# Three products of half-length chunk sets in place of one product of all chunks, and page loads moved from POOL to SP

## The chip, the cores and the metric

The kernel runs on one core of a Trainium2 chip. The metric is the device time of one execution in microseconds (us), as the median of three runs. TensorE is PE, VectorE DVE, ScalarE ACT, GpSimd POOL and SyncE SP in what follows. All arithmetic is in float32; PE takes a float32 product in two passes, and the profile lists each pass as one MATMUL with its LDWEIGHTS.

## The reference, cut to what matters

One step of a hybrid decoder layer: projection, retention, sparse attention for a prompt of 1024 tokens and for 8 sampled tokens (each with 2048 past tokens in 16 pages of a cache), output projection, feed-forward. What the change touches is the compression of the cached rows: blocks of 32 tokens that start every 16 tokens go through a small network, for keys (k) and values (v).

```python
def compress(rows, pos_emb, w1, w2):
    L = rows.shape[0]
    nb = (L - CMP_BLK) // CMP_STRIDE + 1
    idx = np.arange(nb)[:, None] * CMP_STRIDE + np.arange(CMP_BLK)[None, :]
    blk = rows[idx] + pos_emb[None, :, None, :]
    blk = blk.transpose(0, 2, 1, 3).reshape(nb, KV_GROUPS, CMP_BLK * HEAD_DIM)
    return jax.nn.gelu(blk @ w1) @ w2
```

The compressed keys give scores, from whose softmax the best blocks of each sequence are chosen; the selected rows (`selk`, `selv`), the window rows and the compressed rows are then attended to.

## The kernel before, in words

The program has six stages, one after the other. Only `stage_sequences` is changed; it is followed by `stage_attention` (the prompt's attention), the output projection and the feed-forward stage.

`stage_sequences` works on nine sequences q: q = 0 is the prompt (64 chunks of 16 tokens, 63 blocks), q = 1 to 8 the samples (128 chunks, 127 blocks). It is written out by hand as a software pipeline of eleven steps, 0 to 10 (`STEPS_B`), in which each engine has its own fixed list of instructions, tied by semaphores. In step s PE does, in this order:

- `compress(s, 0)`: the keys' compression of sequence s. Sixteen transposes (`turn_rows`, L1066) bring the chunks' rows into PSUM in four parts i, ACT copies each part into `XT` (`keep_turned`, L1219), and PE multiplies it with the weights `w1` (L1085): 32 products of 254 columns, 64 passes, for q = 0 of 126 columns. Block n is chunk n times the lower half of `w1` plus chunk n+1 times the upper half. ACT then makes the gelu (L1228), and PE the second layer (`compressed`, L1106 and L1111), which comes early in the next sequence's `compress`.
- `values(s-2)`: transposes of the weights of the softmax (L1120), `first_keys` (L1142), and 21 products with the selected and window values (L1129); it signals `pv_done`.
- `scores(s-1)`: transposes of the selected keys (L1142) and the scores (L1165).
- `compress(s, 1)`, the same for values, with `importance(s-1)` (L1171) in its middle.

After `importance`, DVE ranks the blocks (L1417 to L1433) and takes a maximum (L1437); then ACT takes two exponentials (L1240, L1250), DVE scales (L1381, L1384, signal `b_scaled`), and `values` of the next step may start.

The pages come by DMA. In step s SP waits for `pv_done` of sequence s-2 and loads the window values (L951, L953), waits for the last key transpose and loads 16 pages of `selk` (L916, 64 KB each), then the window keys (L959), then reads the 16 page numbers of sequence s+2 into registers (L936), waits until POOL has regrouped the blocks before, and loads that sequence's 16 pages of 128 KB into `cmpb` (L916). POOL loads the 16 pages of `selv` (L983, `load_values`) and regroups `cmpb` into `cmpg` (L1003). In step 0 SP also loads the retention state of the samples and a table of constants. After the last step SP loads `kstage` (L966) and the queries (L846) for the next stage.

At the start DVE also normalizes the prompt's retention output (L1316 to L1325), and, once the state and the constants are there, computes the samples' retention (L1330 to L1347), which needs a square root by ACT (L1282) in its middle.

## Time and profile before

| what | value |
|---|---|
| median of 3 runs | 2133.79 us (2131.57 to 2135.72) |
| the profiled execution | 2134.98 us, its span 2133.3 us |
| PE busy over the span | 94% |
| DVE, ACT, POOL busy | 38%, 30%, 28% |
| `stage_sequences` | from 461.6 to 942.4 us of the span |

A row of the trace gives start, duration, engine, line, operation, what it writes and reads, and how many instructions were merged; in brackets the idle time of the engine before it and what ended it. The trace's granted clock of PE is 1.00 at its upper level, 2.4 GHz, and 0.50 at its lower, 1.2 GHz.

### The profile page before, as it was taken

To read this page: it belongs to the slowest core of one execution; us is meant where nothing else is said; L and a number is where in the kernel's file an instruction comes from. 1 tells how busy PE (TensorE), PEld (TensorE's weight loads), DVE (VectorE), ACT (ScalarE), POOL (GpSimd) and SP (SyncE) were. 2 spreads that over 40 slices of the span, in tenths; PEclk is the share of its full clock that TensorE was granted. 3 is DMA by queue.
4 is the path that set the end of the run, shared out by engine and by line. 5 is a ranking of instruction groups with operands and counts; after the bars stand their busy time and mean duration, and the time that the engine had idled before them with its cause. 6 is when DMAs were issued, how large, how long until landed. Compare 5 with 4: busy or idle time off the path is not lost. (4 is left out here: it accounts for less than half of the span.)

```text
span 2133.3 us, 32535 instructions
## 1 busy us (share of the span) xinstructions
PE 1997.9 (94%) x11749; PEld 1729.3 (81%) x11749; DVE 817.4 (38%) x1590; ACT 637.6 (30%) x1290; POOL 600.0 (28%) x628
## 2 busy tenths in 40 slices
PE   6999989977999999869999989899999999999997
PEld 4777767855777777647778868699999999999987
DVE  5634443454354344467777843101111101110115
ACT  4301111212233334356777843222101111111112
POOL 0111111211232222154545731133322323223330
PEclk9999989988999999979999989999999999999999
DMA  6121101247786784470000032211111111111113
GB/s 182 42 89 40 40 12 61 81 133 117 109 110 97 102 100 66 57 154 13 11 11 21 2 99 90 70 49 44 45 49 49 39 49 43 45 49 49 45 64 120
DMA packets 173848, 141.33 MB, mean 66 GB/s; under 512 B 16601, under 2 KB 160682, under 8 KB 173410
## 3 DMA queue, kind: packets, MB, share of 16 engines
q1 hardware_dynamic: 169634, 131.43, 26.9%
q0 software_dynamic: 4096, 8.40, 2.6%
q8 instruction: 66, 1.08, 0.2%
q14 instruction: 52, 0.43, 0.1%
HBM read 124.27 MB, written 19.69 MB: 67 GB/s over the span
## 5 line engine op out<-in xcount | busy, mean ns | idle before, releaser
L392 PE MATMUL banks<-halves 128*128 128x344 f32 (+4 forms) x5184 | 855.1, 327 | 14.4 <-POOL halves L401 14.4
L392 PEld LDWEIGHTS banks<-halves 128*128 128x128 f32 (+1 forms) x5184 | 820.6, 188 | 44.8 <-POOL halves L401 7.7
L401 POOL TENSOR_TENSOR halves<-core,halves 128x1024 fp32r<-128x1024 f32 (+1 forms) x143 | 243.9, 1713 | 574.9 <-ACT halves L397 425.0
L392 PE MATMUL banks<-hidden 128*128 128x512 f32 (+3 forms) x1512 | 349.4, 387 | 9.0 <-DVE hidden L401 9.0
L392 PEld LDWEIGHTS banks<-hidden 128*128 128x128 f32 (+1 forms) x1512 | 254.5, 179 | 77.5 <-issue 9.7
L1085 PE MATMUL banks<-arena,blocks 128*128 128x254 f32 (+1 forms) x1152 | 248.2, 372 | 9.1 <-ACT arena L1219 5.1
L1085 PEld LDWEIGHTS banks<-arena,blocks 128*128 128x128 f32 x1152 | 209.4, 194 | 34.4 <-issue 6.1
L397 ACT ACTIVATE halves<-core 128x1024 fp32r<-128x1024 f32 (+1 forms) x85 | 88.1, 1047 | 390.3 <-PE banks L392 369.6
L2063 DVE TENSOR_TENSOR core<-banks,core 128x344 f32<-128x344 f32 x66 | 34.1, 517 | 440.4 <-PE banks L392 440.4
L1653 POOL TENSOR_SCALAR arena<-arena,kept 128x64 f32<-128x64 f32 (+8 forms) x192 | 123.3, 654 | 129.3 <-DVE arena L1705 127.2
L983 POOL DMA_DIRECT2D arena<-in_cache_kv x128 | 67.9, 530 | 232.6 <-PE banks L1129 206.0
L1694 DVE TENSOR_REDUCE arena<-banks 128x1 f32<-128x64 f32 (+8 forms) x184 | 101.6, 557 | 61.7 <-PE banks L1577 58.1
L1619 ACT ACTIVATE arena<-banks,arena 128x64 f32<-128x64 f32 (+8 forms) x192 | 109.3, 570 | 47.9 <-DVE arena L1694 46.4
L1573 PEld LDWEIGHTS banks<-pairs 128*128 128x128 f32 x592 | 98.9, 197 | 25.0 <-ACT arena L1619 16.2
L1573 PE MATMUL banks<-pairs 128*128 128x128 f32 (+3 forms) x592 | 105.4, 310 | 9.8 <-ACT arena L1619 9.1
L1601 PE MATMUL banks<-pairs 128*128 128x512 f32 (+1 forms) x296 | 106.2, 440 | 3.4 <-ACT arena L1640 3.4
L1586 PE MATMUL banks<-core,arena 128*128 128x128 f32 (+1 forms) x592 | 94.0, 282 | 11.1 <-DVE pairs L401 10.1
L596 POOL TENSOR_TENSOR retention<-core,retention 128x256 f32<-128x256 f32 (+1 forms) x36 | 30.3, 842 | 261.6 <-ACT core L579 261.6
L401 DVE TENSOR_TENSOR pairs<-banks,pairs 128x512 fp32r<-128x512 f32 (+1 forms) x148 | 99.2, 678 | 10.4 <-ACT pairs L397 10.3
L397 ACT ACTIVATE pairs<-banks 128x512 fp32r<-128x512 f32 (+1 forms) x148 | 88.0, 594 | 41.4 <-PE banks L1586 40.6
L1219 ACT ACTIVATE arena<-banks 128x512 f32<-128x512 f32 (+1 forms) x72 | 39.5, 574 | 151.7 <-PE banks L1066 151.2
L664 DVE TENSOR_TENSOR retention<-core,retention 128x128 f32<-128x128 f32 (+1 forms) x72 | 37.6, 564 | 119.9 <-ACT core L579 119.9
(209 smaller groups left out, 1884.6 us busy)
## 6 DMA issues: line engine op xcount, KB each, us to landing
core<-in_cache_kv SPq DMA_DIRECT2D x128, 128.0 KB, 5.3
core<-in_w_gate SPq DMA_DIRECT2D x22, 512.0 KB, 3.7
core<-in_w_up SPq DMA_DIRECT2D x22, 512.0 KB, 3.8
core<-in_x_prompt SPq DMA_DIRECT2D x16, 512.0 KB, 3.4
arena<-in_cache_kv SPq DMA_DIRECT2D x128, 64.0 KB, 6.0
arena<-in_cache_kv POOLq DMA_DIRECT2D x128, 64.0 KB, 5.1
retention<-in_w_in SPq DMA_DIRECT2D x16, 448.0 KB, 6.3
core<-in_w_down SPq DMA_DIRECT2D x16, 448.0 KB, 3.7
```

The lines of the kernel that those rows point to most:

```text
L392: done = pe.matmul(out, left[a], right[b], start=(first and i == 0), stop=(last and i == 2))
L397: return act.activation(hi, x, ACT.Copy)
L401: return engine.tensor_tensor(lo, x, hi.bitcast(F32), ALU.subtract)
L983: pool.dma_start(m.selv[16 * at:16 * at + 16, half, :, :], io.pool[bass.ds(page[pg], 1), :, :, 384:512].rearrange("a c t n -> (a c) t n")) ...
L1085: last = pe.matmul(m.banks[:, 2 + mt, 0:2 * nb], m.w1[kv][:, k, P * mt:P * mt + P], m.XT[:, k % 8, :, k // 8:k // 8 + nb], start=(k == 0), ...
L1219: act.activation(m.XT.rearrange("p (h j) g c -> p j h g c", h=2)[:, i, :, :, 0:nch], m.banks[:, u % 2, :].rearrange("p (g c h) -> p h g c" ...
L1573: last = pe.matmul(out[:, lo:hi], m.qs[t % 2][:, g, hh, :], pair[v][:, first + lo:first + hi], start=(v == 0), stop=(v == 1 and not mask))
L1586: last = pe.transpose(m.banks[0:w, 4 + i % 3, P * hh:P * hh + P], m.prob[(4 * k + hh) % 12][:, P * x:P * x + w], m.ident)
L1601: last = pe.matmul(m.banks[:, 7, :], v.rearrange("p v d -> p (v d)"), m.pts[i % 3][half][0:w, :], start=(br == 0 and half == 0), stop=(br ...
L1619: act.activation(m.prob[u % 12][:, 0:n], scores_of(u), ACT.Exp, bias=m.nmax[:, u % 8:u % 8 + 1], accum_out=m.sums[t % 2][:, u % PER_TILE:u ...
L1653: pool.tensor_scalar(p, p, m.share[t % 2][:, u % PER_TILE:u % PER_TILE + 1], m.gates[:, tile_at(t), gate:gate + 1], ALU.mult, ALU.mult).th ...
L1694: dve.tensor_reduce(peak, scores_of(u), AX.X, ALU.max, negate=True).then_inc(s["c_max"], 1)
```

## The change

It computes the first layer with three products of half as many columns. The chunks are split into even and odd ones. With L and U the lower and upper half of the weights, p1 = odd x L and p0 = even x U, and both = (even + odd) x (L + U). Even blocks are both - p1 - p0, odd blocks p1 plus p0 shifted by one chunk. POOL makes L + U once per kind (`weight_sum`) and even + odd in four parts per sequence and kind (`chunk_sums`), PE makes 48 products of 128 columns (of 64 for q = 0), ACT copies the three results from PSUM to SBUF (`keep_apart`), DVE combines them (`summed`), and ACT makes the gelu from SBUF. Compressed blocks are stored with even ones first, and the mask and the importance sums follow that order. The 16 loads of `selv` go from POOL to SP, behind the window values and ahead of `selk`. On DVE the normalization's second half (`norm_gate`) goes behind the samples' retention; on ACT the square root goes ahead of the copies of `compress(0, 1)`; on PE `compressed` and `importance` go further back in `compress`.

```diff
@@ -94,7 +94,7 @@
-    n = np.arange(64)
+    n = 2 * (np.arange(64) % 32) + np.arange(64) // 32
...
@@ -256,13 +256,16 @@
-    m.XT = b(2048).rearrange("p (j g c) -> p j g c", j=8, g=2)
+    m.XT = b(2048)
+    m.both = b(1024).rearrange("p (j g c) -> p j g c", j=8, g=2)
+    m.w1sum = [e(2048).rearrange("p (k n) -> p k n", k=8) for _ in range(2)]
+    m.apart, m.hidden = e(768), e(512).rearrange("p (e n) -> p e n", e=2)
...
@@ -882,6 +885,12 @@
+    even, odd = (m.XT[:, 1024 * e:1024 * e + 1024].rearrange("p (j g c) -> p j g c", j=8, g=2) for e in range(2))
+
+    def products(ap, q):
+
+        return ap.rearrange("p (a c) -> p a c", c=64)[:, :, 0:chunks_of(q) // 2]
...
@@ -951,6 +960,7 @@
                     sp.dma_start(m.winv, io.wins[q - 1, :, :].rearrange("(p t) n -> p t n", t=4)[:, :, 128:256]
                                  ).then_inc(s["last_values_in"], 16)
                     sp.dma_start(m.vcb[q % 2][127:128, :], io.kvs[q - 1:q, 384:512]).then_inc(s["last_values_in"], 16)
+                    pages(q, m.selv, 384, 128, "values_in")
...
@@ -971,38 +981,45 @@
-            def load_values(q):
-                for pg in range(NPG):
-                    half, at = divmod(pg, NPG // 2)
-                    pool.dma_start(m.selv[16 * at:16 * at + 16, half, :, :],
-                                   io.pool[bass.ds(page[pg], 1), :, :, 384:512].rearrange("a c t n -> (a c) t n")
-                                   ).then_inc(s["values_in"], 16)
...
+            def regroup(q, kv):
+                n = CH if q else HCH
+                if q:
+                    pool.wait_ge(s["cmp_in"], 16 * NPG * q)
+                    pool.wait_ge(s["b_turned"], TURN_AT["kv"[kv], q - 1, 3] + 1)
+                pool.tensor_copy(m.cmpg[:, kv, :, 0:n, :],
+                                 m.cmpb.rearrange("p h t n -> p (h t) n")[:, 0:n, P * kv:P * kv + P]
+                                 .rearrange("p t (g d) -> p g t d", g=2)).then_inc(s["b_grouped"], 1)
+
+            def weight_sum(kv):
+                pool.wait_ge(s[f"b_w_in{kv}"], 48 if kv else 128)
+                pool.tensor_tensor(m.w1sum[kv], m.w1[kv][:, 0:8, :], m.w1[kv][:, 8:16, :], ALU.add).then_inc(s["b_w_sum"], 1)
+
+            def chunk_sums(q, kv):
+                mc = chunks_of(q) // 2
+                for i in range(4):
+                    pool.wait_ge(s["b_kept_act"], kept_by(TURN_AT["kv"[kv], q, i] + 1, False))
+                    out, x0, x1 = (x.rearrange("p (h j) g c -> p j h g c", h=2)[:, i, :, :, 0:mc] for x in (m.both, even, odd))
+                    pool.tensor_tensor(out, x0, x1, ALU.add).then_inc(s["b_both"], 1)
 
             pool.wait_ge(s["cmp_early"], 16)
...
-                if q >= 3:
-                    load_values(q - 2)
...
+            regroup(0, 0)
+            regroup(0, 1)
+            pool.wait_ge(s["b_w_first"], 64)
+            weight_sum(0)
+            for step in STEPS_B:
+                for kv in range(2):
+                    if step in SEQS_B and (step or kv == 0):
+                        chunk_sums(step, kv)
+                    if step == 0 and kv == 0:
+                        weight_sum(1)
+                        chunk_sums(0, 1)
+                    if step == 2 and kv == 0:
+                        pool.wait_ge(s["b_kc_kept"], 1)
+                        nb = chunks_of(0) - 1
+                        rest_to_lo(pool, m.kcbP[:, :, 1, 0:nb], m.kcb[0].rearrange("p (g n) -> p g n", g=2)[:, :, 0:nb],
+                                   m.kcbP[:, :, 0, 0:nb]).then_inc(s["b_kcp_lo"], 1)
+                    if step + 1 in SEQS_B:
+                        regroup(step + 1, kv)
...
@@ -1066,29 +1083,47 @@
+                def product(bank, at, w, x, j, mt, first):
+                    out = m.banks[:, bank, at:at + P].rearrange("p (g c) -> p g c", g=2)[:, :, 0:mc]
+                    return pe.matmul(out, w[:, P * mt:P * mt + P], x[:, j, :, 0:mc], start=first, stop=(j == 7),
+                                     skip_group_check=True)
+
+                def shared(i):
+                    if q == 0 and i == 0:
+                        pe.wait_ge(s["b_w_sum"], kv + 1)
+                    pe.wait_ge(s["b_both"], 8 * q + 4 * kv + i + 1)
+                    for j in (i, 4 + i):
+                        for mt in range(2):
+                            last = product(3, P * mt, m.w1sum[kv][:, j, :], m.both, j, mt, j == mt == 0)
+                    return last
+
+                mc = nch // 2
                 turn_rows(0)
                 turn_rows(1)
-                if kv == 0 and q:
-                    compressed(q - 1)
-                done = 2 * q + kv
-                if q == 0 and kv:
-                    pe.wait_ge(s["b_w_in1"], 48)
-                wait(pe, "b_gelu", 2 * done)
+                wait(pe, "b_apart", 2 * (2 * q + kv))
                 for i in range(4):
                     if i in (1, 2):
                         turn_rows(i + 1)
-                    if done == 0 and i % 2 == 0:
+                    if q == 0 and i == 0 and kv:
+                        pe.wait_ge(s["b_w_in1"], 48)
+                    if q == 0 and i % 2 == 0 and kv == 0:
                         pe.wait_ge(s["b_w_in0" if i else "b_w_first"], 128 if i else 64)
                     pe.wait_ge(s["b_kept_act"], kept_by(TURN_AT["kv"[kv], q, i] + 1, False))
-                    for k in (i, 4 + i, 8 + i, 12 + i):
+                    for j in (i, 4 + i):
                         for mt in range(2):
-                            last = pe.matmul(m.banks[:, 2 + mt, 0:2 * nb], m.w1[kv][:, k, P * mt:P * mt + P],
-                                             m.XT[:, k % 8, :, k // 8:k // 8 + nb], start=(k == 0), stop=(k == 15))
-                    if i == 0 and kv == 1 and 1 <= q - 1:
+                            product(2, P * mt, m.w1[kv][:, j, :], odd, j, mt, j == mt == 0)
+                            last = product(2, 256 + P * mt, m.w1[kv][:, 8 + j, :], even, j, mt, False)
+                    if i == 3:
+                        last.then_inc(s["b_apart_done"], 1)
+                    if i:
+                        shared(i - 1)
+                    if i == 1 and kv == 0 and q:
+                        compressed(q - 1)
+                    if i == 1 and kv == 1 and 1 <= q - 1:
                         if 1 <= q - 2:
                             turn_output(q - 2)
                         importance(q - 1)
-                last.then_inc(s["b_hidden"], 1)
+                shared(3).then_inc(s["b_hidden"], 1)
                 if q == 0:
                     position_bias(kv)
...
@@ -1210,23 +1245,34 @@
-                nch = chunks_of(q)
+                mc = chunks_of(q) // 2
-                    act.activation(m.XT.rearrange("p (h j) g c -> p j h g c", h=2)[:, i, :, :, 0:nch],
-                                   m.banks[:, u % 2, :].rearrange("p (g c h) -> p h g c", g=2, h=2)[:, :, :, 0:nch],
+                    act.activation(m.XT.rearrange("p (x j g c) -> p j x g c", x=4, j=4, g=2)[:, i, :, :, 0:mc],
+                                   m.banks[:, u % 2, :].rearrange("p (g c x) -> p x g c", g=2, x=4)[:, :, :, 0:mc],
                                    ACT.Copy).then_inc(s["b_kept_act"], 1)
 
+            def keep_apart(q, kv):
+                n = 2 * q + kv
+                act.wait_ge(s["b_apart_done"], n + 1)
+                wait(act, "b_summed", n)
+                act.activation(products(m.apart[:, 0:512], q), products(m.banks[:, 2, :], q), ACT.Copy).then_inc(s["b_apart"], 1)
+                act.wait_ge(s["b_hidden"], n + 1)
+                act.activation(products(m.apart[:, 512:768], q), products(m.banks[:, 3, 0:256], q), ACT.Copy
+                               ).then_inc(s["b_apart"], 1)
-                act.wait_ge(s["b_hidden"], 2 * q + kv + 1)
+                mc = chunks_of(q) // 2
+                act.wait_ge(s["b_summed"], 2 * q + kv + 1)
-                    act.activation(m.G[kv][:, mt, 0:2 * nb], m.banks[:, 2 + mt, 0:2 * nb], ACT.Gelu_apprx_tanh,
-                                   bias=m.cbias[:, 2 * mt + kv:2 * mt + kv + 1]).then_inc(s["b_gelu"], 1)
+                    act.activation(m.G[kv][:, mt, 0:4 * mc].rearrange("p (g e c) -> p g e c", g=2, e=2),
+                                   m.hidden[:, :, P * mt:P * mt + P].rearrange("p e (g c) -> p g e c", g=2)[:, :, :, 0:mc],
+                                   ACT.Gelu_apprx_tanh, bias=m.cbias[:, 2 * mt + kv:2 * mt + kv + 1]
+                                   ).then_inc(s["b_gelu"], 1)
...
@@ -1252,7 +1298,12 @@
                 if step == 0:
                     keep_bias(0)
                 if step in SEQS_B:
+                    keep_apart(step, 0)
                     gelu(step, 0)
+                if step == 0:
+                    act.wait_ge(s["r_ssum"], 1)
+                    act.activation(rms, ss, ACT.Sqrt, bias=m.small[0:NR, 64:65], scale=1.0 / HD
+                                   ).then_inc(s["r_srms"], 1)
...
@@ -1274,13 +1325,12 @@
                     keep_turned(q, 1, range(2 if 1 <= q - 1 <= NB_SEQ else 0, 4))
                     if q == 0:
                         keep_bias(1)
+                    keep_apart(q, 1)
+                    if q + 1 in SEQS_B:
+                        keep_turned(q + 1, 0, range(2))
                     gelu(q, 1)
                     if q + 1 in SEQS_B:
-                        keep_turned(q + 1, 0)
-                    if q == 0:
-                        act.wait_ge(s["r_ssum"], 1)
-                        act.activation(rms, ss, ACT.Sqrt, bias=m.small[0:NR, 64:65], scale=1.0 / HD
-                                       ).then_inc(s["r_srms"], 1)
+                        keep_turned(q + 1, 0, range(2, 4))
...
@@ -1311,41 +1361,71 @@
-            for hp in range(4):
+            dve.memset(m.hidden, 0.0).then_inc(s["b_cleared"], 1)
+            dve.wait_ge(s["b_cleared"], 3)
+
+            def summed(q, kv):
+
+                n, last = 2 * q + kv, chunks_of(q) // 2 - 1
+                dve.wait_ge(s["b_apart"], 2 * n + 2)
+                wait(dve, "b_gelu", 2 * n)
+                p1, p0, both = (products(m.apart[:, 256 * x:256 * x + 256], q) for x in range(3))
+                first, second = (products(m.hidden[:, e, :], q) for e in range(2))
+                dve.tensor_tensor(second[:, :, 0:last], p1[:, :, 0:last], p0[:, :, 1:last + 1], ALU.add)
+                own.after(dve.tensor_tensor(first, both, p1, ALU.subtract))
+                dve.tensor_tensor(first, first, p0, ALU.subtract).then_inc(s["b_summed"], 1)
+
+            def norm_sums(hp):
...
-            for hp in range(4):
+
+            def norm_gate(hp):
...
+
+            def sample_out():
+                dve.wait_ge(s["const_in"], 48)
+                dve.wait_ge(s["r_rows_in"], 32)
...
+                dve.tensor_reduce(ss, prod, AX.X, ALU.add).then_inc(s["r_ssum"], 1)
+
+            def sample_state():
...
+                dve.wait_ge(s["r_srms"], 1)
+                own.after(dve.reciprocal(rstd, rms))
+                dve.scalar_tensor_tensor(out=ro, in0=ro, scalar=rstd, in1=rg, op0=ALU.mult, op1=ALU.mult
+                                         ).then_inc(s["r_o"], 1)
+                dve.scalar_tensor_tensor(out=S0, in0=S0, scalar=m.gone[0:NR, :], in1=S2, op0=ALU.mult,
+                                         op1=ALU.add).then_inc(s["r_new_state"], 1)
...
+            for hp in range(4):
+                norm_sums(hp)
+            sample_out()
+            summed(0, 0)
+            sample_state()
+            summed(0, 1)
+            for hp in range(4):
+                norm_gate(hp)
             dve.wait_ge(s["r_gated"], 4)
-
...
+            summed(1, 0)
+            summed(1, 1)
...
@@ -1382,6 +1462,8 @@
                     dve.tensor_scalar(SR[:, SEL], SR[:, SEL], bst[:, 8:9], None, ALU.mult).then_inc(s["b_scaled"], 1)
+                    if step in SEQS_B:
+                        summed(step, 0)
                     dve.wait_ge(s["pt_done"], q)
...
@@ -1397,6 +1479,8 @@
                         keep_output(q)
+                if step == 2:
+                    summed(2, 0)
                 q = step - 1
...
@@ -1434,6 +1518,8 @@
                     own.after(added)
+                    if step in SEQS_B:
+                        summed(step, 1)
                     dve.tensor_reduce(bst[:, 5:6], SR[:, SEL], AX.X, ALU.max, negate=True).then_inc(s["b_sel_max"], 1)
 
 

```

In the listings of order below the line numbers are those of each kernel. First ACT, at the start of `stage_sequences`, from the bias of the keys on. Before (L1196 and L1198 the bias, L1228 gelu, L1219 `keep_turned`, L1282 the square root):

```order
L1196 ACTIVATE arena<-banks 1x256
L1198 ACTIVATE arena<-banks 128x2
L1228 ACT_TABLE_LOAD
L1228 ACTIVATE arena<-banks,arena 128x126 x2
L1219 ACTIVATE arena<-banks 128x2x2x64 x4
L1196 ACTIVATE arena<-banks 1x256
L1198 ACTIVATE arena<-banks 128x2
L1228 ACTIVATE arena<-banks,arena 128x126 x2
L1219 ACTIVATE arena<-banks 128x2x256 x4
L1282 ACT_TABLE_LOAD
L1282 ACTIVATE core<-core 64x1
```

Now ACT at the same place (L1262 and L1264 `keep_apart`, L1272 gelu, L1305 the square root, L1254 `keep_turned`):

```order
L1231 ACTIVATE arena<-banks 1x256
L1233 ACTIVATE arena<-banks 128x2
L1262 ACTIVATE blocks<-banks 128x8x32
L1264 ACTIVATE blocks<-banks 128x4x32
L1272 ACT_TABLE_LOAD
L1272 ACTIVATE arena<-blocks,arena 128x128 x2
L1305 ACT_TABLE_LOAD
L1305 ACTIVATE core<-core 64x1
L1254 ACTIVATE arena<-banks 128x4x2x32 x4
```

The gelu of `compress(0, 0)` now waits for DVE's `summed(0, 0)`, and it and the square root stand ahead of the four copies that `compress(0, 1)` multiplies.

Now DVE at the same place, behind the four pairs of `norm_sums` (L1395 to L1406 `sample_out`, L1374 to L1376 `summed(0, 0)`, L1409 the start of `sample_state`):

```order
L1395 TENSOR_SCALAR core<-core 64x64
L1396 TENSOR_TENSOR core<-core 64x64
L1397 TENSOR_REDUCE core<-core 64x1
L1398 TENSOR_SCALAR core<-core 64x64
L1400 TENSOR_TENSOR arena<-arena,core 64x4096
L1402 TENSOR_REDUCE core<-arena 64x64
L1403 SCALAR_TENSOR_TENSOR core<-core,arena 64x64
L1405 TENSOR_TENSOR core<-core 64x64
L1406 TENSOR_REDUCE core<-core 64x1
L1374 TENSOR_TENSOR blocks<-blocks 128x4x31
L1375 TENSOR_TENSOR blocks<-blocks 128x4x32
L1376 TENSOR_TENSOR blocks<-blocks 128x4x32
```

The whole of `sample_out` stands ahead of `summed(0, 0)`; before, nothing that the compression waits for stood on DVE.

## Rows read from the trace of the kernel before

**Rows 1.** Groups by line and shape; 40 us of steady steps: busy PE, PEld, DVE, ACT, POOL, clock.

```profile
L1085 PE MATMUL banks<-arena,blocks 128*128 128x254 f32 x1024 | 230.4, 381 | 3.4 <-ACT arena L1219 3.4
...
L1219 ACT ACTIVATE arena<-banks 128x512 f32<-128x512 f32 x64 | 36.6, 598 | 128.7 <-PE banks L1066 128.3
...
700.00:740.00 40.00, 38.66 (x227) 28.89 (x226) 21.28 (x34) 17.28 (x30) 12.65 (x18) 1.00 0.78 94
```

**Rows 2.** PE in order of time: passes of 254 and 126 columns, transposes and their weight loads.

```profile
731.30 7.02 PE L1085 MATMUL banks<-arena,blocks 128*128 128x254 f32 x32
...
474.40 3.73 PE L1085 MATMUL banks<-arena,blocks 128*128 128x126 f32 x32
...
720.67 0.86 PEld L1066 LDWEIGHTS banks<-core,blocks 128*128 128x128 f32 x8 [0.86 <-issue]
```

**Rows 3.** The start of the stage, in order of time: DVE, ACT, PE.

```profile
487.40 0.62 ACT L1228 ACTIVATE arena<-banks,arena 128x126 f32<-128x126 f32 x2
496.19 7.07 PE L1025 MATMUL banks<-blocks,arena 128*1 128x256 f32 x32
512.05 1.94 PE L1066 MATMUL banks<-core,blocks 128*128 128x128 f32 x8 [8.06 <-issue]
517.42 0.19 DVE L1330 TENSOR_SCALAR core<-core 64x64 f32<-64x64 f32 x1 [29.89 <-DMA arena<-in_const]
518.42 7.30 DVE L1335 TENSOR_TENSOR arena<-arena,core 64x4096 f32<-64x4096 f32 x1
530.76 0.21 DVE L1341 TENSOR_REDUCE core<-core 64x1 f32<-64x64 f32 x1
```

**Rows 4.** Stretch by stretch: the granted clock (0.51) after PE has stood for 8 us.

```profile
512.00:521.00 9.00, 8.95 (x35) 7.94 (x36) 3.44 (x5) 1.20 (x2) 1.79 (x1) 0.51 0.73 180
```

**Rows 5.** SP's DMA issues over one step.

```profile
714.13 0.60 SPq L951 DMA_DIRECT2D core<-out  x1
718.17 11.76 SPq L916 DMA_DIRECT2D arena<-in_cache_kv  x16
729.97 0.60 SPq L959 DMA_DIRECT2D core<-out  x1
740.34 11.86 SPq L916 DMA_DIRECT2D core<-in_cache_kv  x16
763.03 0.60 SPq L951 DMA_DIRECT2D core<-out  x1
```

**Rows 6.** POOL's issues and regrouping in that step, DVE beside it, a POOL addition by group.

```profile
714.79 9.80 POOL L983 DMA_DIRECT2D arena<-in_cache_kv  x16 [29.80 <-PE banks L1129]
724.59 1.90 POOL L1003 COPY blocks<-core 128x2048 f32<-128x2048 f32 x1
...
724.71 1.87 DVE L1409 TENSOR_SCALAR core<-arena,core 8x127 f32<-8x127 f32 x1
...
L596 POOL TENSOR_TENSOR retention<-core,retention 128x256 f32<-128x256 f32 x32 | 26.7, 833 | 234.3 <-ACT core L579 234.3
```

**Rows 7.** Time to landing of the pages that SP loads, from the DMA part of the page.

```profile
core<-in_cache_kv SPq DMA_DIRECT2D x128, 128.0 KB, 5.3
```

**Rows 8.** The last sequence: from the products' end to `pv_done`.

```profile
616.14 0.38 PE L1165 MATMUL banks<-core,kept 128*8 128x128 f32 x2
...
861.46 0.58 SPq L951 DMA_DIRECT2D core<-out  x1
...
893.87 2.40 PE L1120 MATMUL banks<-core,arena 8*128 8x8 f32 x21 [6.34 <-DVE arena L1384]
...
903.68 0.59 SPq L951 DMA_DIRECT2D core<-out  x1
```

**Rows 9.** The end of the stage.

```profile
904.83 4.97 SPq L966 DMA_DIRECT2D core<-turned_keys  x8
...
920.36 3.89 ACT L397 ACTIVATE pairs<-core 128x1024 fp32r<-128x1024 f32 x4
924.15 1.99 ACT L1250 ACTIVATE arena<-arena,core 8x2049 f32<-8x2049 f32 x1
```

More of the change, by code:

```diff
@@ L280, in place_mixer @@
     m.rrow = x(512)
-    m.G = [b(508).rearrange("p (m n) -> p m n", m=2) for i in range(2)]
+    m.G = [b(512).rearrange("p (m n) -> p m n", m=2) for i in range(2)]
     m.brow = b(256)
@@ L973, in _ @@
         def _(pool):
-            def load_values(q):
-                page = [pool.value_load(m.pages[0:1, x:x + 1], min_val=0, max_val=NPOOL - 1)
-                        for x in range(NPG * (q - 1), NPG * q)]
-                if q == 1:
-                    pool.wait_ge(s["r_new_state"], 1)
-                wait(pool, "pv_done", q - 1)
-                for pg in range(NPG):
-                    half, at = divmod(pg, NPG // 2)
-                    pool.dma_start(m.selv[16 * at:16 * at + 16, half, :, :],
-                                   io.pool[bass.ds(page[pg], 1), :, :, 384:512].rearrange("a c t n -> (a c) t n")
-                                   ).then_inc(s["values_in"], 16)
@@ L1334, in _ @@
-            dve.wait_ge(s["r_state_in"], 16)
-            own.after(dve.tensor_tensor(S2v, S0v.rearrange("p d e -> p e d"), rq.unsqueeze(1).broadcast_to(S2v.shape),
-                                        ALU.mult))
-            own.after(dve.tensor_reduce(qs, S2v, AX.X, ALU.add))
-            own.after(dve.scalar_tensor_tensor(out=ro, in0=qs, scalar=m.gone[0:NR, :], in1=ro, op0=ALU.mult,
-                                               op1=ALU.add))
-            own.after(dve.tensor_tensor(prod, ro, ro, ALU.mult))
@@ new lines, in sample_state @@
+            def sample_state():
+                own.after(dve.tensor_tensor(S2v, rk8.unsqueeze(2).broadcast_to(S2v.shape),
+                                            rv.unsqueeze(1).broadcast_to(S2v.shape), ALU.mult))
+                dve.wait_ge(s["r_srms"], 1)
[4 more added lines that the diff above has]
+                                         op1=ALU.add).then_inc(s["r_new_state"], 1)
```

52 lines of the change are left out of this document (16 added, 36 removed).

## The prediction, made blind

> **What bounds the kernel now.** I read the groups by line first, to find which engine `stage_sequences` waits for. In 40 us of steady steps PE is busy for 38.66 us at the full clock, DVE for 21.28, ACT for 17.28, POOL for 12.65 [rows 1]. So PE sets the pace of these steps, and the passes of the first layer (1024 of them) are the largest piece of its work. PE in order of time gives their real spacing, which the mean of 381 ns in the group does not, since passes overlap: 32 passes of 254 columns take 7.02 us, so one takes 0.2145 us once the last one's tail is taken off [rows 2]. Then SP in order of time: one step lasts from 714.13 to 763.03, 48.9 us, and SP's first issue in it comes as soon as `pv_done` is there [rows 5]. The start and the end of the stage are different: there PE stands, for the first sample's blocks [rows 3] and for DVE and ACT at the last sequence [rows 8]. They have to be followed one by one.
>
> **The passes.** A `compress` of a sample had 64 passes of 254 columns, 13.7 us. It now has 96 of 128. The nearest row is 32 passes of 126 columns in 3.73 us, 0.111 us each [rows 2]; with two more columns 0.112, so 96 take 10.7 us. The gain is 3.0 us each, 48 us over sixteen. From below the stream of 128 columns can't be under half of 0.2145, which would give 10.3 us; from above I allow 0.125, 12 us. For q = 0 it is the other way: 64 passes of 126 columns took 7.1 us, 96 of 64 columns each still load 128 columns of weights, and a load takes 0.106 us (eight in 0.86 us) [rows 2], so I take 0.11, 10.6 us: 3.5 us more each, where PE is waited for at all.
>
> The rows of 126 columns show the load running beside the stream: 0.111 us holds a load of 0.106 and a stream of 0.105. The Trainium skill, page "TensorE: Matmul & The Clock Gate", section "The mechanism", says that a weight load overlaps running products only where the row groups differ. By that rule the new passes would cost the sum, about 0.21 us, and sixteen `compress` would lose 6.7 us each instead of gaining 3.0. The row is against it.
>
> **The start.** This is where I expect the largest single loss. DVE could begin the samples' retention only at 517.42, when the constants had landed, and came to the end of what is now `sample_out` at 530.76 + 0.21 = 530.97 [rows 3]. Nothing in the change brings that data earlier: SP issues it behind the first sample's pages, as before. Now `summed(0, 0)` stands behind `sample_out` on DVE, the gelu of `compress(0, 0)` waits for it, and on ACT the gelu and the square root stand ahead of the copies for `compress(0, 1)`. ACT issues in order, so PE gets no part of `compress(0, 1)` until then. Step by step: three small DVE operations to 531.9 (0.3 each); gelu 0.6 (before, 0.62 [rows 3]); a table load of 1.28 and the root 0.3; the first copy 0.4: 534.4. Before, that gelu ran at 487.40. Then `compress(0, 1)`: PE has stood for 40 us. After the 8.06 us of standing before 512.05, the clock stood at 0.51 for the next 9 us [rows 3, 4]; so 9 us of the passes go at half speed (41 passes), the other 55 take 6.1 us, transposes 0.4: 550. The bias takes 7.07 [rows 3] and 0.9 for its copies: `compress(1, 0)` begins at 558.0 instead of 512.05, **46 us later**. The wait for the first pages (8.06) and POOL's weight sums are hidden in this.
>
> **From there to the first `pv_done`.** It stood at 616.3 [rows 8]. Five `compress` lie between, 15.0 us less. The slow 9 us after 512.05 cost 4.3 and are not paid again. New waits: `compress(1, 1)` follows at once, and its first copy stands behind PSUM copies (0.5), `summed` (1.2) and gelu (0.8) on ACT, 2.5 us; `scores(1)` waits 1.0 for `summed(2, 0)`; 0.4 at each start of a `compress(s, 0)` for `keep_apart`: 4.7 together. So `pv_done` of sequence 1 comes at 616.3 + 46 - 15.0 - 4.3 + 4.7 = 647.7.
>
> **A steady step by PE alone** would be 48.9 - 2 x 3.0 + 0.2 = 43.1 us. The copies (0.60 for 512 columns [rows 1]) and POOL's additions (0.83 for 256 columns [rows 6], four per `compress`) fit beside 1.8 us of passes per part.
>
> **SP's step.** From the first load of `selk` at 718.17 to the end of the `cmpb` issues at 752.20 SP has no wait on PE: 34.0 us, of which 9.8 are the reading of page numbers between 730.57 and 740.34 [rows 5]. The window values add 1.2. The change adds 16 issues of the kind that took 11.76 us. That is 34.0 + 1.2 + 11.8 = **47.0 us in a step**, more than PE's 43.1: SP becomes the pace-setter as long as it still has `cmpb` to load, in steps 3 to 6. It starts level (its step 2 ends at about 645), so `cmpb` of sequence 8 is issued by 647.7 + 4 x 47.0 = 835.7. The last page lands 5.3 us after its issue [rows 7], 4.6 after that; regrouping takes 1.90, the first addition 0.83 [rows 6]: 843.0. The wait is felt at the first shared product of `compress(7, 1)`, because on POOL the regrouping of sequence 8 stands ahead of the additions for it; that product lies 12.4 us behind `pv_done` of sequence 5, which is thus at 830.6 in effect, and `pv_done` of sequence 6 at 830.6 + 43.1 = 873.7. Before, it was at 861.4 [rows 8].
>
> What POOL is relieved of, 9.80 us of issues [rows 6], was waited for by nobody: `selv` is used 30 us later. The Trainium skill, page "SBUF — State Buffer", section "SBUF: two separate sides", warns that DVE copies stop DMAs issued from POOL and advises issuing them elsewhere. By that rule the move is a gain; the sum would be the same by it, less at most a few us at the last sequence, where nothing waits for these loads either.
>
> **The last sequence.** From `pv_done` 6 to `pv_done` 7 took 903.68 - 861.46 = 42.2 us [rows 8], with PE waiting 6.34 us for DVE at the end. The saved passes don't help: the ranking starts 1.1 us later (`importance` stands further back), `summed(8, 1)` adds 1.2 to it, and the gelu comes just behind. I get the same 42.2: 915.9, 12.2 us later than before.
>
> **The end.** SP issued `kstage` right behind the window values, at 904.83 for 4.97 us; ACT rounded it at 920.36 for 3.89 us and made the last exponential at 924.15 [rows 9]. Now 11.8 us of `selv` issues stand ahead: issued up to 18.0 us after `pv_done`, landed at 23.5, rounded by 27.4, exponential from there, against 20.5 before. **6.8 us** that nothing covers; the values that DVE and POOL prepare for the next stage hang on it.
>
> **Sum:** 12.2 + 6.8 = 19.0 us on the profiled execution's 2134.98, 2154.0. The profiled one is 1.2 above the median, so I forecast a median of **2153 us**. The later stages have the same work.
>
> **The rivals.**
> - SP does not set the pace: an issue of `selv` is cheaper than one of `selk`, or the page numbers are read faster. Then the five steps take 43.1: 647.7 + 5 x 43.1 + 42.2 = 905.4, 1.7 later than before, and with the end 2143.5. Against it: the 16 issues took the same 0.74 us each for 64 and 128 KB [rows 5]. 14%.
> - The start is covered, the other sign: `compress(0, 1)` does not wait for `sample_out`. It decides at 487.4, when PE would take the first copy. Then `pv_done` 1 is at about 604. With SP's pace SP is then at 628 after step 2 and `cmpb` 8 at 816, and the end comes out at -7 + 7: 2135. With PE's pace it is 604 + 215.5 + 42.2 = 861.7, 42 earlier, 2100. For it only that the data might land sooner; the order rows speak against it. 5% and 4%.
> - It is worse by contention: an operation of 0.27 us on DVE took 1.87 beside POOL's copy [rows 6], and POOL now works beside DVE's ranking and `summed`. With 2 us more in each of seven steps the sum is 2168. 15%.
> - Loads don't hide behind passes of 128 columns. Sixteen times 6.7 instead of -3.0 puts it at 2134 + 46 + 107, less what the start saved, about 2280. 1%, since the row of 126 columns is so near.
>
> **How the numbers follow.** The forecast has the other 61%, with a range of its own of 2146 to 2162 from 0.107 to 0.125 a pass (half of it hidden behind SP) and 46 to 48.5 for SP's step. The range of 8 in 10 reaches to the second and the fourth case: 2138 to 2169. About 4 us, 0.2%, is what a measurement can tell: faster 5%, the same 8%, slower 87%.
>
> **What the changed profile would show.** PE idle from about 492 to 534, ending at an ACT copy; 96 passes per `compress` at 0.112 us; SP issuing without a gap between 648 and 836, and `pv_done` every 47 us; PE waits of some 4 us at `compress(s, 1)` for POOL's additions; ACT waiting for `kstage` at the end. I am wrong if PE doesn't stand at 490, or if SP waits for `pv_done` in steps 4 to 6.

## The result and the profile after

| what | value |
|---|---|
| the changed kernel | 2184.99 us, median of 4 runs (2184.33 to 2187.1) |
| the kernel before, on the same chip | 2134.76 us (2131.57 to 2137.15) |
| ratio | 1.0238, 95% interval 1.022 to 1.0256 |
| span of the profiled execution | 2185.3 us (before 2133.3) |

The change makes the kernel 50 us slower. I had forecast slower, but by 19 us (2153, range 2138 to 2169): the direction is right and the size is not.

In the rows of the changed kernel L1083 are the transposes of `turn_rows`, L1088 the passes of the first layer, L1042 the bias, L1254 the copies of `keep_turned`, L1002 POOL's additions (`chunk_sums`), L989 its regrouping and L925 the page loads.

The groups by line and shape from 560 to 700 us of the changed kernel:

```profile
L1088 PE MATMUL banks<-arena,blocks 128*128 128x128 f32 x672 | 79.0, 276 | 4.8 <-ACT arena L1254 4.8
L1254 ACT ACTIVATE arena<-banks 128x512 f32<-128x512 f32 x28 | 15.9, 593 | 24.6 <-PE banks L1083 24.2
```

The windows (busy PE, PEld, DVE, ACT, POOL, then the granted clock, the DMA share and GB/s):

```profile
482.00:494.00 12.00, 12.00 (x59) 12.00 (x57) 0.00 (x0) 2.57 (x6) 4.91 (x2) 0.50 0.07 17
544.00:556.00 12.00, 12.00 (x58) 11.90 (x56) 0.00 (x0) 0.39 (x1) 4.12 (x3) 0.50 0.45 65
574.40:580.00 5.60, 5.60 (x52) 5.60 (x51) 5.50 (x5) 1.67 (x5) 4.56 (x2) 1.00 0.29 86
760.00:800.00 40.00, 33.69 (x276) 31.45 (x275) 21.12 (x34) 14.45 (x26) 11.40 (x10) 0.87 0.60 92
```

Beside [rows 1] the last window is the one to look at: there PE is no longer busy throughout, and its clock is 0.87 instead of 1.00. It is the worst of the steady steps; from 700 to 760 and from 800 to 855 us the clock is 0.97.

The waits of PE over this stage, as in the list of waits (us in total, times, longest):

```profile
PE banks L1088 <- ACT arena L1254: 38.2, 17, 29.7
PE banks L1155 <- issue: 17.1, 1, 17.1
PE banks L1088 <- POOL arena L1002: 14.2, 5, 5.1
PE banks L1141 <- ACT arena L1272: 7.6, 5, 4.9
```

The start in order of time on PE; it answers to [rows 2, 3]:

```profile
504.33 0.66 PE L1083 MATMUL banks<-core,blocks 128*128 128x128 f32 x4 [0.26 <-ACT arena L1233]
534.73 3.65 PE L1088 MATMUL banks<-arena,blocks 128*128 128x64 f32 x16 [29.75 <-ACT arena L1254]
...
544.04 12.05 PE L1088 MATMUL banks<-arena,blocks 128*128 128x64 f32 x56
556.01 8.90 PE L1042 MATMUL banks<-blocks,arena 128*1 128x256 f32 x32
...
565.92 1.09 PE L1083 MATMUL banks<-core,blocks 128*128 128x128 f32 x8 [0.26 <-ACT arena L1233]
```

And on DVE and ACT:

```profile
474.06 1.22 DVE L1381 TENSOR_REDUCE core<-arena 128x16 f32<-128x1024 f32 x1
517.89 0.19 DVE L1395 TENSOR_SCALAR core<-core 64x64 f32<-64x64 f32 x1 [42.62 <-DMA arena<-in_const]
...
531.19 0.27 DVE L1374 TENSOR_TENSOR blocks<-blocks 128x124 f32<-128x124 f32 x1
...
532.02 0.69 ACT L1272 ACTIVATE arena<-blocks,arena 128x128 f32<-128x128 f32 x2 [25.86 <-DVE blocks L1376]
```

DVE stood for 42.62 us for the constants, with the first `summed` (L1374) queued behind them in program order; ACT stood for that sum, and PE for ACT. PE took up work at 534.73.

SP over one step, which answers to [rows 5]:

```profile
806.12 1.06 SPq L960 DMA_DIRECT2D core<-out  x1
807.23 0.51 SPq L962 DMA_DIRECT2D core<-out  x1
807.92 25.06 SPq L925 DMA_DIRECT2D arena<-in_cache_kv  x32
833.03 0.60 SPq L969 DMA_DIRECT2D core<-out  x1
843.41 11.85 SPq L925 DMA_DIRECT2D core<-in_cache_kv  x16
855.30 0.60 SPq L960 DMA_DIRECT2D core<-out  x1
```

There is no gap but the reading of page numbers (833.63 to 843.41), so SP does not wait for `pv_done` in this step. L960 comes at 658.66, 708.68, 757.04, 806.12 and 855.30, 49.2 us a step. Behind SP's last `cmpb` issue come POOL and PE:

```profile
862.75 1.89 POOL L989 COPY blocks<-core 128x2048 f32<-128x2048 f32 x1 [27.99 <-DMA core<-in_cache_kv]
864.60 2.08 POOL L1002 TENSOR_TENSOR arena<-arena 128x256 f32<-128x256 f32 x3
```

```profile
865.37 2.07 PE L1088 MATMUL banks<-arena,blocks 128*128 128x128 f32 x8 [3.81 <-POOL arena L1002]
869.00 8.70 PE L1088 MATMUL banks<-arena,blocks 128*128 128x128 f32 x56
```

The data is there at 862.75; PE then stands 3.81 us for an addition of the present sample, queued behind the regrouping of the next, and its 56 passes take 8.70 us instead of 6.42 after that stop. The end:

```profile
900.49 0.58 SPq L960 DMA_DIRECT2D core<-out  x1
945.52 0.58 SPq L960 DMA_DIRECT2D core<-out  x1
959.72 5.07 SPq L976 DMA_DIRECT2D core<-turned_keys  x8
...
971.15 3.89 ACT L400 ACTIVATE pairs<-core 128x1024 fp32r<-128x1024 f32 x4 [9.05 <-DMA core<-turned_keys]
```

ACT waits 9.05 us for `kstage`.

### The profile page after: what moved, and what is told of

Read it like the earlier page. It is cut to its first block and busy times, and to the rows that moved or that the text cites. A ratio compares the mean times of both kernels' runs of the same rounds, so it can differ in the third digit from the quotient of the medians.

```text
span 2185.3 us, 33508 instructions
## 1 busy us (share of the span) xinstructions
PE 1994.9 (91%) x12325; PEld 1746.4 (80%) x12325; DVE 846.3 (39%) x1645; ACT 654.5 (30%) x1326; POOL 599.6 (27%) x574
## 5 line engine op out<-in xcount | busy, mean ns | idle before, releaser
L1088 PE MATMUL banks<-arena,blocks 128*128 128x128 f32 (+1 forms) x1728 | 229.5, 297 | 57.1 <-ACT arena L1254 38.2
L1088 PEld LDWEIGHTS banks<-arena,blocks 128*128 128x128 f32 x1728 | 223.1, 212 | 61.9 <-issue 41.7
L1659 PEld LDWEIGHTS banks<-pairs 128*128 128x128 f32 x592 | 100.1, 200 | 24.4 <-ACT arena L1705 15.6
L1002 POOL TENSOR_TENSOR arena<-arena 128x256 f32<-128x256 f32 (+1 forms) x72 | 58.7, 829 | 208.0 <-ACT arena L1254 208.0
L2100 ACT ACTIVATE core<-banks 128x344 f32<-128x344 f32 x66 | 30.3, 460 | 175.0 <-PE banks L395 174.9
```

What stands on the lines that cost most here:

```text
L1002: pool.tensor_tensor(out, x0, x1, ALU.add).then_inc(s["b_both"], 1)
L1088: return pe.matmul(out, w[:, P * mt:P * mt + P], x[:, j, :, 0:mc], start=first, stop=(j == 7), skip_group_check=True)
L1659: last = pe.matmul(out[:, lo:hi], m.qs[t % 2][:, g, hh, :], pair[v][:, first + lo:first + hi], start=(v == 0), stop=(v == 1 and not mask))
```

## The experiments

Theory: the loss is made by queues, not by products. DVE's at the start, SP's in the middle and at the end, and POOL's where additions stand behind a regrouping. Rival: the three-product form costs it by itself (clock, contention, copies, sums). Twelve kernels separate them. Ratios are to the kernel before, measured on the same chip as each; its medians there lay between 2135.1 and 2137.0. Line numbers shift by some between kernels.

| run | median us | ratio (interval) |
|---|---|---|
| e1_start | 2188.09 | 1.0249 (1.0219 to 1.0279) |
| e2_pool_values | 2191.79 | 1.0256 (1.0223 to 1.029) |
| e3_both | 2199.61 | 1.0295 (1.0264 to 1.0325) |
| e4_sp_only | 2143.56 | 1.0036 (1.0021 to 1.005) |
| e5_wide | 2176.91 | 1.0197 (1.0171 to 1.0223) |
| e6_regroup_late | 2177.45 | 1.0207 (1.0181 to 1.0234) |
| e8_start3 | 2153.65 | 1.0089 (1.0063 to 1.0115) |
| e10_start3_late | 2148.95 | 1.0062 (1.0041 to 1.0083) |
| e9_start3_pool_late | 2132.81 | 0.9986 (0.9973 to 0.9999) |
| e12_start3_pool | 2163.65 | 1.0137 (1.0116 to 1.0159) |
| e11_all_wide | 2136.08 | 1.0003 (0.999 to 1.0017) |
| e13_all_wide2 | 2127.28 | 0.9958 (0.9941 to 0.9975) |

### e1: another order at the start

```diff
-            sample_out()
             summed(0, 0)
-            sample_state()
             summed(0, 1)
             for hp in range(4):
                 norm_gate(hp)
+            sample_out()
+            sample_state()
             summed(1, 0)
```

The square root on ACT goes back behind the copies of `compress(1, 0)`.

> The changed kernel with the start in another order: on DVE summed(0, 0), summed(0, 1) and the four norm_gate stand ahead of sample_out, and ACT's square root goes back behind the copies of compress(1, 0). If ACT's wait for sample_out holds PE at the start, the wait of 29.75 us before the first passes of compress(0, 1) is gone and compress(1, 0) begins about 33 us earlier (near 533 instead of 565.9). If SP sets the pace behind that, not all of it comes out at the end: SP's chain of loads can only start some 20 to 24 us earlier, so the median falls from 2185 to about 2162. If SP does not set the pace, all 33 come out: 2152. If PE stands at the start for another reason, nothing changes: 2185.

2188.09: a miss. PE in order of time:

```profile
504.28 2.61 PE L1088 MATMUL banks<-arena,blocks 128*128 128x64 f32 x16 [2.29 <-ACT arena L1254]
...
534.95 1.09 PE L1083 MATMUL banks<-core,blocks 128*128 128x128 f32 x8 [0.26 <-ACT arena L1233]
...
575.31 3.75 PE L1088 MATMUL banks<-arena,blocks 128*128 128x128 f32 x16 [24.56 <-ACT arena L1254]
```

`compress(1, 0)` began 31 us earlier, and 24.56 us of standing came back one product later. `summed(1, 0)` was now queued behind the gates (536.25 to 550), the sample's output (550.01 to 563.38) and its state, while DVE had stood idle for the 32.7 us before 535.5. PE's waits for POOL's additions grew too, to 21.7 us from 14.2, and nothing of the earlier start was left at the end. Moving a wait is not removing it; the gap in which DVE has nothing to do has to be filled.

### e2, e3: the loads of the selected values back on POOL

```diff
-                    pages(q, m.selv, 384, 128, "values_in")     # SP
+                    if kv == 1 and 1 <= step - 1 <= NB_SEQ:     # POOL
+                        load_values(step - 1)
                     if step in SEQS_B and (step or kv == 0):
                         chunk_sums(step, kv)
```

e3 has both edits.

> The changed kernel with the 16 loads of selv given back to POOL, behind regroup(step + 1, 0) and ahead of the additions of compress(step, 1). If SP's issues set the pace from sequence 3 on, its waits for pv_done come back in every step, PE's waits for POOL's additions (1.6, 5.1, 1.3 and 3.8 us) go and with them the slow clock behind them: steps of 44 us, 22 us earlier at the last pv_done; kstage follows the window values again, 8 us more at the end: about 2155. If the move to SP costs only the end, 2177. If it costs nothing, 2185.

> Both edits. If start and SP's pace are two separate losses in a row, they hide each other in neither kernel alone: 33 + 22 + 8 = 63 us less than the changed kernel, about 2122, faster than before by the passes saved. If the passes of 128 columns don't pay as the trace says, it stays at 2134 or above.

2191.79 and 2199.61: misses again. POOL in e2:

```profile
716.35 1.89 POOL L988 COPY blocks<-core 128x2048 f32<-128x2048 f32 x1 [14.07 <-DMA core<-in_cache_kv]
725.74 8.57 POOL L1000 DMA_DIRECT2D arena<-in_cache_kv  x14 [7.50 <-issue]
734.70 1.15 POOL L1000 DMA_DIRECT2D arena<-in_cache_kv  x2 [0.40 <-issue]
735.87 2.09 POOL L1013 TENSOR_TENSOR arena<-arena 128x256 f32<-128x256 f32 x3
```

The regrouping waits for its DMA, then 7.5 us go into reading page numbers and 9.7 into issues, and only then come the additions. PE waited 32.5 us for them, against 14.2. At the end, though, the loss was gone: the next stage began 38.8 us after the last `pv_done`, 47.6 in the changed kernel and 39.2 before the change. In the place tried here POOL's queue is worse than SP's; that says nothing on another place.

### e4: the loads alone moved to SP, in the kernel before

```diff
-                if q >= 3:
-                    load_values(q - 2)                          # POOL
+                    pages(q, m.selv, 384, 128, "values_in")     # SP
```

> The kernel before with only the 16 loads of selv moved to SP (the compression as before). SP's step would be some 49 us, PE's is 48.9, and the regrouping has a later deadline here, since no additions stand behind it on POOL. If the pace matters only where it is above PE's, there are no new waits in the steady steps and only the end is longer, by 8 us: about 2143. If the issues on SP hurt by themselves (queue, contention), it is 2155 or more.

2143.56: as forecast. SP goes at 49.0 us a step (630.60 to 826.60), just PE's old pace. `pv_done` of sequence 6 comes 0.4 us later than before the change (861.81) and that of sequence 7 1.5 us later (905.13), and the next stage begins 46.6 us after that instead of 39.2. So the move costs 8 us, nearly all of it at the end.

### e5: the prompt's products at 128 columns

```diff
-                mc = nch // 2
+                mc = 64
```

(in `compress` and `chunk_sums` for q = 0, with `XT` cleared first)

> The changed kernel, but the prompt's two products take 128 columns a pass (half of them zeros) instead of 64; nothing else moves. Theory A (the clock stays at its lower level because 64-column passes leave the array mostly idle between weight loads): in the prompt's products the granted clock rises above 0.50, the group of 56 passes takes 6.4 to 9 us instead of 12.05, and since only the second of them (and the bias behind it) lies on the path, the time falls by 4 to 8 us, to 2177 to 2181 us. Theory B (the clock is low there because the engine had stood for 30 us and the ramp takes its time, whatever the passes are): the groups keep 12 us (128 columns at half clock are 0.22 us a pass, as 64 were), and the time stays at 2185 us.

2176.91, 8.1 us less, for theory A. The same stretches, PE and the granted clock:

```profile
535.09 3.75 PE L1088 MATMUL banks<-arena,blocks 128*128 128x128 f32 x16 [36.67 <-ACT arena L1254]
...
541.89 6.42 PE L1088 MATMUL banks<-arena,blocks 128*128 128x128 f32 x56
548.24 7.07 PE L1042 MATMUL banks<-blocks,arena 128*1 128x256 f32 x32
```

```profile
482.00:494.00 12.00, 12.00 (x81) 9.24 (x80) 0.00 (x0) 2.57 (x6) 5.20 (x2) 0.90 0.06 11
...
540.00:548.00 8.00, 8.00 (x74) 8.00 (x73) 2.22 (x1) 0.39 (x1) 7.16 (x4) 1.00 0.00 0
```

Twice the columns took half the time: 6.42 us for 56 passes instead of 12.05, at 1.00 (2.4 GHz) instead of 0.50 (1.2 GHz). Both had the same kind of wait ahead of them (36.67 and 29.75 us), so it isn't the wait that kept the clock down. In e8, below, PE had stood only 2.29 us; there the clock went from 0.86 (504.9 to 507.0) down to 0.50 (507.3 to 524.7) while PE was busy with passes of 64 columns throughout, and 56 of them took 12.05 us again. So 8 of the 50 us do come from the new products themselves, as the rival above has it.

### e6: both regroupings behind the additions

```diff
-                    if step + 1 in SEQS_B:
-                        regroup(step + 1, kv)
+                    if step + 1 in SEQS_B and kv:
+                        regroup(step + 1, 0)
+                        regroup(step + 1, 1)
```

> The changed kernel, but GpSimd regroups both halves of the next sample behind the additions of compress(step, 1), not one of them ahead of them, so that no addition waits for a cache DMA. Theory A (the sync engine's chain is late, and the steps are long because the additions are queued behind a regroup that waits for its DMA): the waits of 1.3 to 5.1 us at the products for L1002 go, with them the slow clock behind them, and the deadline of the cache loads moves some 8 us later; 2171 to 2178 us. Theory B (the sync engine alone sets the pace of the middle, 49.2 us a step, and the wait only moves to the turns of the next sample): within 3 us of 2185.

2177.45, 7.5 us less, for theory A. PE's waits for additions fell from 14.2 to 3.0 us. SP's own pace did not change (658.67 to 855.59, again 49.2 us a step); what changed is how late its last `cmpb` may be: `pv_done` of sequence 6 came at 894.04, not 900.49.

### e8: the gates in DVE's idle stretch

```diff
+            for hp in range(4):
+                norm_gate(hp)
+            dve.wait_ge(s["r_gated"], 4)
+            summed(0, 0)
             sample_out()
-            summed(0, 0)
             sample_state()
             summed(0, 1)
-            for hp in range(4):
-                norm_gate(hp)
-            dve.wait_ge(s["r_gated"], 4)
             summed(1, 0)
```

(the square root on ACT behind the copies of `compress(0, 1)`)

> The changed kernel with another order on VectorE at the start: the four gates of the retention output (13.8 us of work) stand ahead of the first sum, in the stretch from 475 to 518 us in which VectorE stood idle; the first sum follows at about 506 us, and only then the sample's output, which waits for its constants until 518. ScalarE's square root stands behind the copies of compress(0,1). Theory A (the start costs 30 us because the first sum is queued behind the sample's output and its DMA): TensorE's wait of 29.8 us shrinks to under 5, compress(1,0) begins at about 540 us instead of 566, and the time is 2155 to 2163. Theory B (the sync engine's later chain absorbs it): the start is earlier by 26 us, but the end by less than 15; above 2170.

2153.65, for theory A and 1.4 us better than its range: 31.3 us less for the order of a few calls.

```profile
504.86 2.22 PE L1088 MATMUL banks<-arena,blocks 128*128 128x64 f32 x16 [2.29 <-ACT arena L1254]
...
533.86 1.09 PE L1083 MATMUL banks<-core,blocks 128*128 128x128 f32 x8 [0.27 <-ACT arena L1233]
```

`compress(1, 0)` begins 32.1 us earlier, and the later chain absorbs none of it.

### e10, e12, e9: late regroupings, loads on POOL, and both

All three have the start of e8; e10 adds e6's edit, e12 that of e2, e9 both.

> The start of the run before, both regroups behind the additions, and the loads of the selected values back on GpSimd, behind the additions of compress(step, 0) and ahead of those of compress(step, 1). If the start (26 us), the sync engine's share (8 us at the end, 2 us a step in the middle) and the regroup's place (8 us) add up: 2130 to 2145 us, near the kernel before or just below it. If GpSimd's issues (9.8 us) ahead of the second additions make TensorE wait, as they did with the regroup between them, 2150 to 2165.

> The new start and both regroups behind the additions, with the loads of the selected values still on the sync engine. If the sync engine's share is what is left between this and the run with the loads on GpSimd as well (the 8 us of the end, and a step that its issues hold at 47 to 49 us in place of 45.5): 2141 to 2151 us. If the sync engine has slack once the start is earlier and the regroups wait later, only the end's 6 to 8 us are left: 2138 to 2141.

> The new start and the loads of the selected values on GpSimd ahead of the additions of compress(step, 1), with one regroup still between them, as in the changed kernel. Theory A (the regroup, which waits for its cache DMA, is what makes the loads on GpSimd harmful, since it stands ahead of loads and additions both): the waits for the additions stay near 30 us in all, and the time is 2155 to 2163 us, no better than with the loads on the sync engine (2153.7). Theory B (the start's wait was what spoiled the first try): 2130 to 2145 us, as with the regroups late.

From e10 to e9 only the queue of the 16 loads differs: 2148.95 and 2132.81, 16.1 us. SP in e10, and then in e9:

```profile
778.18 0.60 SPq L960 DMA_DIRECT2D core<-out  x1
...
779.52 24.89 SPq L925 DMA_DIRECT2D arena<-in_cache_kv  x32
...
826.70 0.60 SPq L960 DMA_DIRECT2D core<-out  x1
```

```profile
768.11 0.60 SPq L960 DMA_DIRECT2D core<-out  x1
...
772.13 13.42 SPq L925 DMA_DIRECT2D arena<-in_cache_kv  x16
...
795.60 11.85 SPq L925 DMA_DIRECT2D core<-in_cache_kv  x16
813.57 0.59 SPq L960 DMA_DIRECT2D core<-out  x1
```

e10 goes at SP's pace, 49.3 us a step from 629.44 to 826.70. In e9 SP waits for `pv_done` again (807.45 to 813.57), and five steps from 631.59 to 859.90 take 45.7 us each, against 48.8 before the change. Those 3.1 us a step are what reaches the end of the 6 us that the passes save, once SP no longer covers them; PE still waits for gelus, 13.7 us in all, and twice 56 passes take 7.8 us instead of 6.42. e12 (2163.65; 33.3 us of waits for additions) confirms theory A of its expectation: with one regrouping still between, the same loads on POOL cost 10 us instead of giving 16.

### e11, e13: everything, with the wide passes

e11 is e9 with e5's edit. e13 also has `summed(0, 1)` ahead of `sample_state` on DVE and the square root behind the copies of `compress(1, 0)` on ACT.

> The new start, the late regroups, the loads on GpSimd and the prompt's products at 128 columns. If the 6 us of the clock add to the rest (the groups of 56 passes at 6.4 us, a bias at 7.1 in place of 8.1 to 9): 2123 to 2129 us, below the kernel before. If another wait of the start (the sample's state, the cache DMAs of the second and third samples) takes their place: 2130 to 2134.

> The run before had TensorE stand 14.0 us at the second bias, since ScalarE's square root, queued ahead of the bias, waited for the sample's output; it took the 6 to 8 us that the wider passes gave. Here the sum of the second product stands between the sample's output and its state on VectorE, and the square root behind the copies of compress(1,0) on ScalarE. If that wait was all that hid the gain: the bias wait is under 1 us, compress(1,0) begins at 527 to 529 us instead of 534, and the time is 2125 to 2131 us, below the kernel before. If the start is earlier and the time is not, the loads of the first sample's values hold it: 2132 to 2137.

e11 gave 2136.08, a miss: above both forecasts, and no gain over e9. The wait is on ACT, then on PE:

```profile
532.93 0.29 ACT L1340 ACTIVATE core<-core 64x1 f32<-64x1 f32 x1 [24.94 <-DVE core L1422]
```

```profile
533.55 0.37 PE L1062 MATMUL banks<-core,arena 1*128 1x1 f32 x2 [14.02 <-ACT arena L1246]
```

PE was done with the second bias sooner and stood 14.02 us, because ACT's copy of it was queued behind a square root that needs the sample's output. In e13 it is not:

```profile
520.49 0.28 PE L1062 MATMUL banks<-core,arena 1*128 1x1 f32 x2 [0.47 <-ACT arena L1246]
521.04 1.09 PE L1098 MATMUL banks<-core,blocks 128*128 128x128 f32 x8 [0.26 <-ACT arena L1248]
```

2127.28, as forecast: 0.42% faster than the kernel before (0.25% to 0.59%). That is a small gain, but e9's interval ends at 0.9999, and e13 is the version whose interval lies clear of 1. `compress(1, 0)` begins 13.1 us earlier than in e11 and 8.8 us of it reach the end; PE now stands 5.00 us for a gelu at 534.69. The two moves were not tried apart.

## Why the prediction was right and wrong

Three terms of the sum failed by most: the clock of the prompt's passes, SP's step, and what lies between SP's last `cmpb` issue and the `pv_done` that waits for it.

- **The passes of 128 columns: right.** 56 passes in 6.42 us is less than 0.115 each, 0.112 with the last one's tail off, at the full clock. The Trainium skill, page "TensorE: Matmul & The Clock Gate", section "The mechanism", has weight loads overlap running products only where the row groups differ. By that rule a pass would take about 0.21 us, and the trace does not bear it out.
- **The wait at the start: right in cause and end, not in length.** It was to end at 534.4 and ended at 534.73, and e8 shows that it was worth 31 us of the time. But I had PE idle from 492, and it stood only from 505, for 29.75 us. By my own sign ("if PE doesn't stand at 490") I was wrong: at 490 PE was in the middle of the 56 passes of `compress(0, 0)` at a clock of 0.50. That cost nothing there, since the constants for DVE set the end of the wait; that the end fits says nothing for the passes ahead of it.
- **The prompt's passes: the first term that failed.** I took 9 us at half speed and full speed after that, from a stretch of other work [rows 4]. The clock stayed at 0.50 through the whole product and rose only in the bias (0.79 from 556 to 565). From the end of the wait to the bias I had 15.6 us and it took 21.3; the bias and its copies took 9.9 instead of 8.0. So `compress(1, 0)` came at 565.92, not 558.0.
- **From there to the first `pv_done`: 3.0 us more** (658.66, not 647.7). Of these, 1.6 are in `values(1)`, whose 32 passes took 4.86 us instead of 3.68, at a clock of 0.75, and 1.4 in `compress(3, 0)`, where PE waits 0.66 us for the gelu and then 0.83 for DVE instead of 0.23. The other differences cancel.
- **SP's step: right mechanism, undersized.** 47.0 us forecast, 49.2 measured, 8.6 us over four steps. I had summed the shortest issues seen in [rows 5]; here 32 took 24.4 to 25.1 us, not 23.5, and 16 of `cmpb` 11.85 to 13.28, and single loads up to 1.35 us instead of 0.60.
- **The coupling of SP, POOL and PE: seen, and undersized by 7.2 us.** From SP's last `cmpb` issue to `pv_done` of sequence 6 I had 38.0 us and it took 45.2. Data came 7.5 us after the last issue instead of 4.6, which is 2.9 of it. The rest is the work behind the wait, which ran at a lower clock (0.50, then 0.72) that I had left out. e6 took most of this away (38.5 us).
- **PE's own step: undersized, hidden behind SP's.** 43.1 us forecast; in e9, where SP waits for PE again, it is 45.7.
- **The last sequence:** 45.0 us instead of 42.2; PE waits 4.94 us for the gelu of `compressed` and runs at a mean clock of 0.81. **The end:** 8.4 us instead of 6.8; the 16 issues ahead of `kstage` took 12.87 us, not 11.8.

In sum: 11.0 at the start, 8.6 + 7.2 in the middle, 2.8 + 1.6 at the end, some 31 us more than forecast until the next stage (942.8 before, 993.1 after: 50.3 measured, 19.0 forecast). No term was wrong in sign. Each was taken at its undisturbed value, and nearly all errors went one way: PE's work went slower at the start and behind the waits, and SP's issues took longer. My contention rival (2 us a step, 2168) had the direction, with 14 of the 31 us that were missing, and not the cause of most of them. The Trainium skill, page "SBUF — State Buffer", section "SBUF: two separate sides", warns that DVE copies hold up DMAs issued from POOL and advises issuing them elsewhere. That did not decide here: moving the loads to SP cost 8 us in e4 and 16 from e9 to e10. No run shows by itself whether DVE held up POOL's issues.

Open: how much of the longer SP issues is due to other traffic, and why data landed later. Neither was tried apart.

## What to carry to other kernels

A saving on the engine that bounds a kernel is worth what the next queue lets through. Before moving work to another engine, add up that engine's step, issues and register reads included, and look at what stands ahead of each new piece in program order: here the order of a few calls decided over 31 us. Fill idle gaps on the helper engine first, since a wait that is only moved comes back later (in e1 one product later, in e11 at the bias). And try edits together as well as alone: the loads on POOL cost 10 us with one placement of a copy (e8 to e12) and gave 16 with another (e10 to e9).

## What the runs showed of the hardware

- Passes of 64 columns on 128 columns of weights ran at a granted clock of 0.50 for as long as they went on (12.05 us for 56), with PE busy all the time; passes of 128 columns in the same place got 0.90 and 1.00, and the second 56 of them took 6.42 us. Half of that wider work was on zeros, and the kernel was 8.1 us faster for it.
- Reading 16 page numbers takes SP 9.4 to 9.8 us, nearly as long as issuing 16 loads (11.8 to 13.3 us); on POOL 7.5 us stood between regrouping and first issue (e2).
- Behind two stops, of 3.8 and 5.1 us, the work went slower: 56 passes took 8.15 us (behind 5.08 at 767.53) and 8.70 us (behind 3.81 at 865.37) instead of 6.42. But the clock also fell where PE had hardly stood: the 32 passes of `values` took 4.86, 5.33 and 5.34 us (from 652.90, 743.94 and 843.04, granted 0.75, 0.67 and 0.67) with no stop over 0.83 us in the 10 us ahead of them. The steady steps before the change had them in 3.68 every time. What brought the clock down there no run shows.
